# Sums of feed-forward weights come from DRAM, conditioning sums move in the second network, and the mixer's first panels are split one by one

## What is computed

```python
def sq_relu_mlp(h, w_up, w_down):
    return jnp.square(jax.nn.relu(h @ w_up)) @ w_down      # w_up 1024x4096, w_down 4096x1024

x = x + fox_mixer(rms_norm(x, ...), ...)                   # first attention
x = x + sq_relu_mlp(rms_norm(x, ...), ...)                 # first network, "ff_a"
x = x + mla_mixer(rms_norm(x, ...), ...)                   # second attention
x = x + sq_relu_mlp(rms_norm(x, ...), ...)                 # second network, "ff_b"
...
mod = (silu(c) @ ada_w + ada_b)                            # conditioning: 1024 -> 6144
y = token_mixer(rms_norm(x, g) * (1 + sc_t) + sh_t, ...)   # its input projection follows ff_b
```

## Time and profile before

| | us |
|---|---|
| Median of three runs (1981.42 to 1982.11) | 1981.95 |
| Profiled execution, its own time | 1981.71 |
| Its span in the profile | 1980.0 |
| TensorE busy | 1961.3 |
| VectorE busy | 1341.7 |
| ScalarE busy | 894.3 |
| DMA, mean rate | 106 GB/s |

### The profile page before, as it was taken

The page is one execution under the profiler, slowest core; times in us unless marked ns, Lnnn a source line. Parts: engine busy times, 40 slices in busy tenths (PEclk is TensorE's granted clock), DMA queues, the critical chain, the costliest instruction groups (busy, mean ns, idle before and its releaser), DMA issues.

```text
span 1980.0 us, 29280 instructions
## 1 busy us (share of the span) xinstructions
PE 1961.3 (99%) x10404; PEld 1640.2 (83%) x10404; DVE 1341.7 (68%) x2145; ACT 894.3 (45%) x1417; POOL 60.4 (3%) x114
## 2 busy tenths in 40 slices
PE   9999999999999999999999999999999999999999
PEld 7777789898987887898988788778888888888888
DVE  6555579687777776797787769574444686563545
ACT  4555554445444554544444443474333544432333
POOL 0000000000110110000001100000000000000000
PEclk9999999999999999999999999999999999999999
DMA  4332243323562114523226513211322412223232
GB/s 158 86 85 85 75 148 129 106 79 98 184 205 78 52 49 157 179 69 106 96 99 214 190 46 104 74 64 65 96 96 98 151 43 85 96 95 105 88 99 91
DMA packets 61292, 209.05 MB, mean 106 GB/s; under 512 B 7160, under 2 KB 10232, under 8 KB 61200
## 3 DMA queue, kind: packets, MB, share of 16 engines
q1 hardware_dynamic: 49920, 168.32, 25.8%
q0 software_dynamic: 10560, 37.28, 6.0%
q10 hardware_dynamic: 720, 2.23, 0.3%
HBM read 205.66 MB, written 2.13 MB: 105 GB/s over the span
## 4 chain that ended last, share of the span: by engine, by line
PE 94%; DVE 4%; ACT 1%; DMA 1%; issue 1%; SPq 0%; DVEq 0%; ACTq 0%
PE bank L893 23%; PE bank L895 23%; PE bank L894 23%; PE bank L1216 4%; PE bank L1218 4%; PE bank L1217 4%; PE bank L1016 1%; PE bank L1091 1%; PE bank L1075 1%; PE bank L998 1%; PE bank L1001 1%; PE bank L1043 1%; PE bank L949 1%; PE bank L951 1%; PE bank L950 1%
## 5 line engine op out<-in xcount | busy, mean ns | idle before, releaser
L893 PE MATMUL bank<-b_hi,w_hi 128*128 128x512 f32 x2060 | 813.0, 395 | 6.6 <-DVE w_lo L2764 4.0
L895 PE MATMUL bank<-b_hi,w_lo 128*128 128x512 f32 x2060 | 802.9, 390 | 0.0
L894 PE MATMUL bank<-b_lo,w_hi 128*128 128x512 f32 x2060 | 802.7, 390 | 0.0
L893 PEld LDWEIGHTS bank<-b_hi,w_hi 128*128 128x128 f32 x2060 | 387.2, 188 | 95.9 <-issue 8.2
L895 PEld LDWEIGHTS bank<-b_hi,w_lo 128*128 128x128 f32 x2060 | 387.0, 188 | 81.0
L894 PEld LDWEIGHTS bank<-b_lo,w_hi 128*128 128x128 f32 x2060 | 387.4, 188 | 80.2 <-issue 2.4
L2764 DVE TENSOR_TENSOR w_lo<-w_raw,w_hi 128x1024 fp32r<-128x1024 f32 (+3 forms) x259 | 306.8, 1185 | 210.2 <-ACT w_hi L1810 209.5
L1810 ACT ACTIVATE w_hi<-w_raw 128x1024 fp32r<-128x1024 f32 (+3 forms) x259 | 265.5, 1025 | 263.3 <-PE bank L895 253.6
L3916 DVE SCALAR_TENSOR_TENSOR arena<-bank,vec,arena 128x511 f32<-128x511 f32 x88 | 65.7, 749 | 85.8 <-ACT arena L2658 80.5
L1216 PE MATMUL bank<-parts,w_hi 128*128 128x256 f32 x384 | 108.7, 283 | 3.3 <-DVE x L3113 3.3
L1218 PE MATMUL bank<-parts,w_lo 128*128 128x256 f32 x384 | 107.9, 281 | 0.0
(11 more groups left out here) (398 smaller groups left out, 2537.9 us busy)
## 6 DMA issues: line engine op xcount, KB each, us to landing
w_raw<-in_wstream SPq DMA_DIRECT2D x253, 512.0 KB, 3.5
arena<-in_ada POOLq DMA_DIRECT2D x48, 512.0 KB, 4.3
plain<-in_wseven SPq DMA_DIRECT2D x24, 512.0 KB, 5.0
early<-in_wseven SPq DMA_DIRECT2D x24, 512.0 KB, 6.8
w_raw<-in_wstream SPq DMA_DIRECT2D x12, 384.0 KB, 3.0
arena<-crow POOLq DMA_DIRECT2D x16, 256.0 KB, 4.8
w_raw<-in_wstream SPq DMA_DIRECT2D x10, 256.0 KB, 2.6
x<-in_xT ACTq DMA_DIRECT2D x4, 512.0 KB, 6.6
```

The lines of the kernel that those rows point to most:

```text
L893: nc.tensor.matmul(dst, whi, rhs_hi(k), start=(k == 0), stop=False)
L894: nc.tensor.matmul(dst, whi, rhs_lo(k), start=False, stop=False)
L895: last = nc.tensor.matmul(dst, wlo, rhs_hi(k), start=False, stop=(k == n - 1))
```

## The change

1. **Sums of weights.** A DRAM tensor `seven_sums` is filled by GpSimd: in each turn one copy of two units' four pieces, and three accumulating DMAs (`accum_op=add`) on the units of the turns before; nine turns for a network, each waiting for all DMAs of the turns before. ff_a's turns stand between the row loads of the first attention, ff_b's behind the sixth early conditioning load in ff_a. SyncE loads each of the 28 weights of a chunk, pieces and sums, by a DMA of 256 KB of its own into a ring of eight; two share a semaphore and a wait. `two`, `three` and `four` go from VectorE.
2. **Conditioning sums.** A third place (the room of the old sums: one data buffer, one row) serves ff_b: in each of its three chunks, a sum at the up tiles 2, 4 and 6 of the group (`tile_condition`) and one in each of units 2 to 4 (`chunk_condition`), 18 in all; six stand in the last six up tiles, none behind the output tiles, and three instead of six in the second attention's output (its output tiles 3 to 5). That output now waits for two row broadcasts (`ada_cin` 64, not 48).
3. **Mixer's first panels.** In ff_b the output tiles are written out by hand: ScalarE's `mix_split` and VectorE's `mix_low` of panel k/2 - 1 follow output tiles k = 2, 4 and 6.

```diff
+        SEVEN_RING = 8
+        GROUP = 2
+        PIECE = (0, None, None, 3, None, None, 2)
+        SUM_AT = (None, 1, 2, None, 0, 3, None)
+        ADA_EARLY, ADA_UP, ADA_POST, ADA_FIRST = 6, 9, 6, 3
...
+            def load_seven(i):
+                if i >= SEVEN_RING and i % GROUP == 0:
+                    sp.wait_ge(seven_lo, seven_count(i - SEVEN_RING + GROUP - 1))
+                n, o = i // SEVEN, i % SEVEN
+                src, at = (seven_rows, PIECE[o]) if PIECE[o] is not None else (sum_rows, SUM_AT[o])
+                sp.dma_start(seven_raw(i), src[n * P:(n + 1) * P, at * T:(at + 1) * T]).then_inc(seven_in[i // GROUP % N_GROUPS], 16)
...
+            def sum_turn(run, turn):
+                first, n = seven_first(run) // SUM_STEP, UNITS // SUM_STEP
+                pool.wait_ge(sum_in, SUM0[run] + 16 * sum(min(max(turn - back, 0), n) for back in range(4)))
+                for back, (to, src, at) in enumerate(((slice(0, 4 * T), seven_rows, slice(0, 4 * T)),
+                                                      (slice(0, 2 * T), seven_rows, slice(T, 3 * T)),
+                                                      (slice(2 * T, 3 * T), sum_rows, slice(0, T)),
+                                                      (slice(3 * T, 4 * T), sum_rows, slice(2 * T, 3 * T)))):
...
+                        if back:
+                            pool.dma_start(sum_rows[units, to], src[units, at], accum_op=ALU.add).then_inc(sum_in, 16)
+                        else:
+                            pool.dma_start(sum_rows[units, to], src[units, at]).then_inc(sum_in, 16)
...
             condition(0, ADA_A, 1)
+            for turn in range(SUM_TURNS):
+                sum_turn("ff_b", turn)
             pool.wait_ge(seven_mm, MM0 + SEVEN * QUAD * SEVEN_CHUNKS)
...
             condition_row(1)
-            condition(ADA_MLA, ADA_B, 1)
+            condition_row(2)
+            condition(ADA_MLA, ADA_MORE, 1)
+            condition(ADA_MORE, ADA_B, 2)
...
-                        if i % SEVEN == 0:
-                            four(at // SEVEN)
-                        if i % SEVEN == 2 and i + 5 < end:
-                            two(at // SEVEN + 1)
-                        if i % SEVEN == 4 and i + 3 < end:
-                            three(at // SEVEN + 1)
+                        if run == "ff_b":
+                            chunk_condition(c, i)
...
+                for k in range(2, KT):
+                    w_split(last + 1 + k)
+                    last_add(k - 1, (k - 1) % 2)
+                    last_post(k - 2, k % 2)
+                    if k % 2 == 0:
+                        mix_low(k // 2 - 1)
```

More of the change, by code:

```diff
@@ L373, in program, with seven_raw @@
         ff_s = [ar(8), ar(9)]
[L377 to L384, removed]
+        SEVEN_RING = 8
+        GROUP = 2
+        N_GROUPS = SEVEN_RING // GROUP
+        PIECE = (0, None, None, 3, None, None, 2)
+        SUM_AT = (None, 1, 2, None, 0, 3, None)
+        UNITS = QUAD * SEVEN_CHUNKS
+        def seven_raw(i):
+            r = i % SEVEN_RING
+            return (plain if r < SEVEN_RING // 2 else early)[:, 2 + r % (SEVEN_RING // 2), :]
         def seven_count(i):
@@ L740, in load_ffn @@
                         sp.wait_ge(free, count)
+                        sp.wait_ge(sum_in, sum_count(run))
                     if c < SEVEN_CHUNKS:
-                        for q in range(QUAD):
-                            load_seven(QUAD * seven_chunk(run, c) + q)
+                        end = SEVEN * QUAD
+                        for i in range(end):
+                            load_seven(end * seven_chunk(run, c) + i)
                 load_panels(at, KT)
@@ L2150, in seven_ffn @@
                 j = first + n - 1
-                def last_square(j):
-                    square(j)
-                    if run == "ff_b":
-                        for p in range(MIX_W):
-                            mix_split(p)
-                segment(run, first + n, KT, last_mid, nothing, lambda: last_square(j), fresh=1)
+                if run == "ff_a":
+                    segment(run, first + n, KT, last_mid, nothing, lambda: square(j), fresh=1)
+                    return last_mid
+                square(j)
+                w_split(first + n + 1)
+                for k in range(2, KT):
+                    w_split(first + n + k)
+                    last_mid(k - 2, k % 2)
+                    if k % 2 == 0:
+                        mix_split(k // 2 - 1)
+                last_mid(KT - 2, 0)
                 return last_mid
@@ L3035, in conditioning, with condition_after @@
                                          accum_out=mod[:, bass.ds(j, 1)]).then_inc(ada_done, 1)
[L3037 removed]
+            def condition_after(post, j0, place, first=0):
                 def both(j, s):
                     post(j, s)
[L3041 to L3042 removed]
+                    if not (isinstance(j, int) and not first <= j < ADA_POST):
+                        conditioning(j + (j0 - first), (s + j0 - first) % 2, place)
                 return both
@@ L3166, in up_tiles @@
                         else:
-                            n0 = QUAD * seven_chunk(run, c)
-                            two(n0)
-                            low(SEVEN * n0)
-                            low(SEVEN * n0 + 1)
-                            three(n0)
+                            low(SEVEN * QUAD * seven_chunk(run, c))
+                            low(SEVEN * QUAD * seven_chunk(run, c) + 1)
                         if not last:
```

151 lines of the change are left out of this document (81 added, 70 removed).

## The result

The changed kernel takes 2018.5 us (median of 4 runs, 2017.12 to 2020.41) against 1981.88 us of the kernel before on the same chip: a ratio of 1.0186, 95% interval 1.0168 to 1.0203. The forecast of 1973.5 us, with a range to 1995, was wrong: the kernel became slower, and by more than the dearest case allowed. The profiled execution took 2019.53 us with a span of 2017.6 us.

What follows compares the result with a forecast made beforehand. TensorE, busy 1961.3 of 1980.0 us, was taken as the bound. Terms -5.6 - 1.0 - 4.65 = -11.3, plus 3 for contention, gave -8.3: 1981.7 to 1973.4, stated as 1973.5 us; range 1969.5 to 1995.

Steps and rivals of the forecast that it cites:

- Sums from DRAM, making them: GpSimd's DRAM turns: free beside the first attention; the second network's slow the first network's chunks, +3 us, bounds 0 and 25.
- rival 1: SyncE's pieces starve beside GpSimd's DRAM traffic at 315 to 441 us, giving about 1998 us; chance 0.20.
- The price of a packet: In the first network's first chunk, each GpSimd packet holds a DMA engine 0.16 us, or 0.24 if accumulating costs twice.
- The pairing: In the first chunk, 105 of SyncE's 160 packets per engine each stand beside one of GpSimd's: 29.6 to 38 us.
- The length: The second network's turns start at 300 us and last 130 to 170 us; the second chunk loses 0 to 2 us.
- Turns beside the first attention: First network's turns between row loads take 17 to 25 us each, end near 200 us, and cost nothing.
- VectorE's relief: Four feed-forward chunks lose their 1.4 us stalls once VectorE no longer makes the weight sums: -5.6 us.
- Rival 3: Chunk stalls come from mixing steps, not sums, and stay: 1979.0 us; chance 0.16 together with contention of 6 to 11 us.
- The loads of single pieces: SyncE fetches 28 pieces of 256 KB per chunk instead of 16; costs nothing on a quiet queue.
- Conditioning sums in the chunks: In the second network's chunks, a 1.3 us sum in units 2 to 4 and reloads of the single buffer cost nothing.
- Output projection: Second attention's output: the first gap stays, with a wait about 1.3 us longer; the second gap goes, -1.0 us.
- The mixer: Spreading the mixer's panel splits over the second network's output tiles removes a 3.05 us gap and 1.6 us lower clock: -4.65 us.

Runs made afterwards that it cites:

- the launch of transfers alone: No computation: six kinds of DRAM-to-DRAM transfer run singly, then beside SyncE's 256 KB loads; a contiguous 2 MB copy took 8.2 us, then 10.4.
- the run with one network: Kernel before plus the change to the mixer's first panels, and DRAM sums for the first network only; the last kernel tried: 1975.14 us, ratio 0.9966.
- without turns: Changed kernel without its 18 turns of DRAM transfers, loading plain weight pieces in place of the sums: 1974.22 us, ratio 0.9962.
- two places: Changed kernel with the second network's turns later, second broadcast not awaited in the output projection, chunk conditioning sums two steps earlier: 1980.3 us, ratio 0.9989.

## Why the prediction was wrong, step by step

**The step that failed** is "Sums from DRAM, making them", for the second network: +3 us with bounds of 0 and 25. Against clean chunks and tiles (39.8, 43.7 and 39.8 us) the changed kernel's 57.1, 50.3 and 58.6 us are 42.7 us too many. The mechanism was there, as rival 1 with a chance of 0.20; the size was wrong in four terms.
- The price of a packet. I took it from loads of 3.6 KB, at most doubled: 0.16 to 0.24 us as a mean. Measured: 0.41 us in 10 us of additions, and 0.663 x 57 x 16 / 1043 = 0.58 us over the first chunk, with its 64 KB packets. My turn had 64 packets per engine; it has 2 + 16 + 32 = 50.
- The pairing. I let each of 105 packets of SyncE's stand beside one of GpSimd's. In the chunk GpSimd's queue had 1043 / 16 = 65 per engine. My formula gives 105 x (0.08 + 0.41) + 4.4 = 55.9 us with the one price and 105 x (0.08 + 0.58) + 4.4 = 73.7 with the other; that the first is near the 57.1 measured is chance. What does add up is the engines' time: 0.663 + 0.337 of 57 us, 37.8 us for GpSimd's queue and 19.2 for SyncE's, with no pause left.
- The length. Full turns of 12 to 20 us were expected (17 to 25 beside the first attention); they take 29 to 30. GpSimd's queue is then not done at 430 to 470 us but at 492, and the second chunk, for which I had 0 to 2 us and in the rival some 5, loses 18.8; the tiles between, for which I had nothing, lose 6.6. This took the time past the range.
- What a stall brings with it. TensorE's four gaps in the first chunk (2.8, 1.2, 1.3 and 7.9 us) are 13.3 us of the 17.3; at the longest two the granted clock falls to its lower level, 1.2 GHz, for 3.4 and 6.8 us, which is the 0.91 of its stretch above and makes the rest. I had priced a lower clock for the mixer but not behind stalls of my own.

The Trainium skill's rule on reducing transfers ("Collectives: The Full Stack", the bandwidth ceiling) gave half the rate. Here 1 MB added took 10.6 us against 6.6 copied, 1.6 times, so the rule is right in kind. The Trainium skill's rule that engines take turns by packet ("DMA: Bandwidth & Descriptors", "Queues, rings and completion order") agrees with 295 packets to 301; the 253 to 571 in the launch of transfers alone are not one to one. The Trainium skill ("DMA: Bandwidth & Descriptors", "SWDGE vs HWDGE vs iDMA") has packets of preferably at most 4096 B; GpSimd's contiguous copy had 64 KB ones, which no row of before could show.

**Turns beside the first attention**: nothing, right; but a full turn takes 28 to 29.4 us where I had 17 to 25 and a bound of 30, and they end at 228 us instead of near 200, so the margin was thinner than it sounded.

**VectorE's relief**: -5.6 us, right. Four chunks went from 41.2 to 39.8 us wherever no turn disturbed them, 5.5 us. Rival 3 (mixing steps) is out, by the run with one network most plainly. The loads of single pieces cost nothing on a quiet queue: right.

**Conditioning sums in the chunks** were taken at nothing, but one of them stands ahead of the next panel's low parts: 0.6 us at each of three chunk ends, 1.8 us. I had looked at the reload of the buffer and at a unit's load, not at what follows the last unit.

**Output projection**: -1.0 us. The second gap is gone, as said. But the wait for two broadcasts was to be 1.3 us longer and is 1.4 to 2.9 us longer (6.4 to 7.9 against 5.0), and in the changed kernel TensorE's first gap grew with it to 2.5 us, with the lower clock behind. The stretch came out at -0.9 us without turns, and at +1.9 us both in the changed kernel and in the one with the first network's turns alone. I had it that the first gap stays.

**The mixer**: -4.65 us forecast, 3.9 measured alone. The gap and the clock are gone as forecast. The forecast had nothing late behind it: 0.45 us comes back inside the first output tile, where TensorE waits for an activation's low part, and in the mixer's part alone 0.26 us in each of three later tiles, where the low part of a mixer panel and a conditioning sum that stays there stand ahead of the tile's own low part. From the end of the second network's third chunk to the end, 920.1 us before are 916.2 with the mixer's part alone and 917.4 in the changed kernel. The latter has the 0.6 us of the sum behind the chunk, and about 1.3 us of a 3.4 us stretch of the lower clock at 1387 us, in the mixer, which two other kernels have (without turns, and two places), and the rest of the kernels here do not.

Left open: why a second broadcast lands between 5.5 and 6.9 us in kernels that are alike up to it, how the first chunk's loss divides between the 64 KB packets and the additions, and whether turns for some of the second network's units, placed between the attention heads only, would add to the last kernel. That was not tried.

## What to carry to other kernels

Work moved from a compute engine to the DMA engines was free here only where the loads beside it had more in hand than they needed under contention: read the landing times and the advance of every load in the window that the new transfers will cover, and not only whether the bytes fit. Price a kind of transfer that the trace does not show by a run of its own before building on it. When its price is a guess, put it where loads are sparse (here between attention heads, where three of four turns cost nothing), and look at the far end of its run as well as its beginning.

## What the runs showed of the hardware

- A contiguous DRAM-to-DRAM copy of GpSimd's went in 64 KB packets, 2.5 to 2.6 us each on an engine; SyncE's queue moved 0.01 MB in 4 us of one.
- DRAM to DRAM, a 4 KB packet added costs 0.39 us of an engine and a 2 KB one 0.19; the same bytes cost alike in either form alone, 10.6 and 10.8 us for 1 MB, but 13.4 and 16.6 us beside a stream of loads.
- A copy of 2 MB in 2 KB rows takes 10.9 us, contiguous 8.2; beside a stream of loads 16.5 and 10.4.
- How two queues share the packets is not fixed: 295 of GpSimd's to 301 of SyncE's in the changed kernel, with six to eight of SyncE's loads and two of GpSimd's additions in flight, but 253 to 571 in the launch of transfers alone, with eight and one. The number of loads in flight does not explain it; the cause is open.
- TensorE's clock can fall without a stall: in the changed kernel the granted clock was 0.50 from 1387.5 to 1390.5 us, in the mixer, with TensorE busy for all of the 11 us before.
